# Order of the work in the attention slots of a hybrid encoder layer, on one Trainium2 core

## What is computed

```
h = RMSNorm(x);  P = h @ W_in, split into q,k,v of branch A; q,k,v of branch B; u of branch C; gate logits
A = softmax attention over a band of 9 chunks of 64 (here: all earlier chunks), relative bias,
    RMS-normed q and k, 8 heads of 64
B = stick-breaking attention, 8 heads of 64: w_ts = sig(z_ts) * prod_{s<j<t} (1 - sig(z_tj)), s < t
C = trailing means over 2/4/8/16 tokens of u, minus u, times a small matrix per group
x = x + W_out( sig(g_A)*(A W_a) + sig(g_B)*(B W_b) + sig(g_C)*(C W_c) )
x = x + W_down( silu(conv(hg)) * conv(hv) ),  [hg|hv] = RMSNorm(x) @ W_up
```

## Time and profile before

| | |
|---|---|
| median of 3 runs | 869.53 us (867.52 to 869.59) |
| the profiled execution | 869.46 us, its span in the trace 867.8 us |
| PE busy | 843.1 us (97%), 3953 matmuls |
| DVE, ACT, POOL busy | 522.5, 388.7, 138.3 us |
| granted TensorE clock, mean | 0.998 |
| DMA | 81.5 MB, mean 94 GB/s |
| slots 0 to 7 and the tail | from about 73 to 345 us of the span |

### The profile page before, as it was taken

The page is one execution under the profiler, slowest core; times in us unless marked ns, Lnnn a source line. Parts: engine busy times, 40 slices in busy tenths (PEclk is TensorE's granted clock), DMA queues, the critical chain, the costliest instruction groups (busy, mean ns, idle before and its releaser), DMA issues.

```text
span 867.8 us, 11900 instructions
## 1 busy us (share of the span) xinstructions
PE 843.1 (97%) x3953; PEld 693.1 (80%) x3953; DVE 522.5 (60%) x715; ACT 388.7 (45%) x557; POOL 138.3 (16%) x118
## 2 busy tenths in 40 slices
PE   5999999999999988999999999999999999999998
PEld 5788777787787777888888888888888888888886
DVE  5435768767467577455554666666666667533334
ACT  6435776655645535343435454333333334322221
POOL 2200222200100133000000312222222222200000
PEclk9999999999999999999999999999999999999999
DMA  6333223221312322333334332333333333222223
GB/s 199 99 97 98 68 78 98 75 71 49 97 48 69 89 72 86 99 93 99 97 95 135 97 97 78 96 96 96 96 96 96 97 96 96 98 97 96 97 97 121
DMA packets 126634, 81.50 MB, mean 94 GB/s; under 512 B 5028, under 2 KB 116360, under 8 KB 126608
## 3 DMA queue, kind: packets, MB, share of 16 engines
q1 hardware_dynamic: 125936, 79.04, 30.1%
q0 software_dynamic: 672, 2.12, 1.0%
HBM read 79.03 MB, written 2.12 MB: 94 GB/s over the span
## 4 chain that ended last, share of the span: by engine, by line
PE 83%; DVE 9%; ACT 3%; issue 2%; POOL 1%; DMA 1%; SPq 1%; ACTq 0%; DVEq 0%; POOLq 0%
PE ps L1182 25%; PE ps L1184 25%; PE ps L1183 25%; DVE suffix L909 2%; PE ps L1257 1%; PE ps L1269 1%; DVE pt_lo L932 1%; PE ps L1283 1%; PE ps L1284 1%; DMA w_raw<-in_w_in_dram 1%; DVE pa L916 1%; PE ps L1236 1%; DVE w_lo L799 1%; DVE out_sb L1172 1%; POOL o_lo L381 1%
## 5 line engine op out<-in xcount | busy, mean ns | idle before, releaser
L799 DVE TENSOR_TENSOR w_lo<-w_raw,w_hi 128x1024 fp32r<-128x1024 f32 x141 | 175.4, 1244 | 182.0 <-ACT w_hi L463 142.7
L1182 PE MATMUL ps<-h_lo,w_hi 128*128 128x512 f32 x704 | 277.4, 394 | 1.4 <-ACT gates L576 0.6
L1184 PE MATMUL ps<-h_hi,w_lo 128*128 128x512 f32 x704 | 274.2, 389 | 0.0
L1183 PE MATMUL ps<-h_hi,w_hi 128*128 128x512 f32 x704 | 274.1, 389 | 0.0
L463 ACT ACTIVATE w_hi<-w_raw 128x1024 fp32r<-128x1024 f32 x126 | 133.6, 1060 | 313.3 <-PE ps L1184 313.2
L1182 PEld LDWEIGHTS ps<-h_lo,w_hi 128*128 128x128 f32 x704 | 132.2, 188 | 28.9 <-issue 2.2
L1184 PEld LDWEIGHTS ps<-h_hi,w_lo 128*128 128x128 f32 x704 | 132.2, 188 | 28.0
L1183 PEld LDWEIGHTS ps<-h_hi,w_hi 128*128 128x128 f32 x704 | 132.3, 188 | 26.5 <-issue 0.2
L1182 PE MATMUL ps<-w_lo,a_hi 128*128 128x512 f32 x176 | 68.5, 389 | 0.0
L1183 PE MATMUL ps<-w_hi,a_hi 128*128 128x512 f32 x176 | 68.5, 389 | 0.0
L1184 PE MATMUL ps<-w_hi,a_lo 128*128 128x512 f32 x176 | 68.5, 389 | 0.0
(11 more groups left out here) (186 smaller groups left out, 1125.3 us busy)
## 6 DMA issues: line engine op xcount, KB each, us to landing
w_raw<-in_w_in_dram SPq DMA_DIRECT2D x104, 256.0 KB, 3.1
w_raw<-in_w_up_dram SPq DMA_DIRECT2D x88, 256.0 KB, 3.1
w_raw<-in_w_down_dram SPq DMA_DIRECT2D x44, 256.0 KB, 2.8
w_raw<-in_w_out_dram SPq DMA_DIRECT2D x16, 256.0 KB, 3.0
x_in<-in_x_dram SPq DMA_DIRECT2D x4, 512.0 KB, 6.3
bias_rev<-rel_bias_rows POOLq DMA_DIRECT2D x8, 256.0 KB, 3.5
x_re<-in_x_dram SPq DMA_DIRECT2D x2, 1024.0 KB, 6.0
w_raw<-in_w_branch_a_dram SPq DMA_DIRECT2D x8, 256.0 KB, 2.7
```

Source lines behind the costliest of these rows:

```text
L799: v.tensor_tensor(w_lo[:, slot, :], w_raw[:, slot, :], r32(w_hi[:, slot, :]), ALU.subtract)\
L1182: mm3(dst, l_hi, r_lo, start=start, stop=False, **kw)
L1183: mm3(dst, l_hi, r_hi, start=False, stop=False, **kw)
L1184: return mm3(dst, l_lo, r_hi, start=False, stop=stop, **kw)
```

## The change

- `o_sum` has a half for each head; `o_part(s, h)` waits for the `o_lo` of the same head one slot earlier.
- TensorE, stick-breaking slots: head 0's transposes stand in the middle of tile b+1, head 0's output and head 1's transposes in the middle of b+2, head 1's output in the middle of b+3. Softmax slots keep their order.
- All slots: the wait for the second gate of the slot before stands ahead of tile b+1 instead of tile b.
- The masks of a slot's scores are added ahead of all scores, not behind each block.
- The split of a slot's values is done at the end of the slot before, by ACT and DVE. ACT's gate copy stands ahead of the rounding of b+5.
- DVE: `sticks` becomes `stick_scan` and `stick_weights`; the second weights come behind the second scan, `lo(b+2)` and head 0's `pt_lo`. The second softmax scaling stands ahead of `pt_lo`, head 0's sum ahead of the Newton steps. ACT's `o_part(s, 0)` stands ahead of `norms_a`.
- POOL begins the pooling sums only when all sixteen heads' weights are done (`p_ready` 16). In the tail mix 0 and 1 follow tile b+4, mix 2 and 3 tile b+5, and `pooled_lo` is a function of its own.
- ACT's and DVE's loops over slots 1 and 2 are written out, and the table preload before ACT's is gone.

The diff, without the changed indices of `o_sum` in other lines and without functions that were only split:

```diff
-            ("o_sum", [P, S], FP32))
+            ("o_sum", [P, 2, S], FP32))
...
                 pool.wait_ge(o_hi_ready, s * 2 + h + 1)
-                pool.tensor_tensor(o_lo[own(h), s, :], o_sum[own(h), :], r32(o_hi[own(h), s, :]), ALU.subtract)\
+                pool.tensor_tensor(o_lo[own(h), s, :], o_sum[own(h), h, :], r32(o_hi[own(h), s, :]), ALU.subtract)\
...
+            pool.wait_ge(p_ready, 16)
             step = 0
...
+            def v_split_hi(s, v, pair):
+                if not (isinstance(s, int) and s == 0):
                     a.wait_ge(pv_done, s * 2)
...
             def o_part(s, h):
                 a.wait_ge(pv_done, s * 2 + h + 1)
-                if not (isinstance(s, int) and s + h == 0):
-                    a.wait_ge(o_lo_ready, s * 2 + h)
-                act(o_sum[own(1 - h), :], ps[own(1 - h), HEAD[h], :], ACT.Copy).then_inc(o_part_ready, 1)
+                if not (isinstance(s, int) and s == 0):
+                    a.wait_ge(o_lo_ready, s * 2 + (h - 1))
+                act(o_sum[own(1 - h), h, :], ps[own(1 - h), HEAD[h], :], ACT.Copy).then_inc(o_part_ready, 1)
...
-            def slot(s, attn, proj):
+            def slot_a(s, proj):
                 b = s * 4 + N_SLOT
...
-                first = isinstance(s, int) and s == 0
-                if attn == "A":
-                    v_split_hi(s, v_a, s, first)
-                    attn_probs(s, 0, attn)
-                    attn_probs(s, 1, attn)
-                else:
-                    attn_probs(s, 0, attn)
-                    attn_probs(s, 1, attn)
-                    v_split_hi(s, v_b, s - 4, False)
+                first = s == 0
                 t = s * 2 + 2
-                if attn == "A":
-                    pt_split_hi(s, 0, first)
+                attn_probs(s, 0, "A")
+                attn_probs(s, 1, "A")
+                pt_split_hi(s, 0, first)
...
-                if attn == "B":
-                    pt_split_hi(s, 0, first)
                 hi_at(b + 2, 0, half + 1)
                 if proj == "A":
                     proj_a(t + 1, 1, PROJ[1], b + 2, True)
+                    o_part(s, 0)
                     norms_a(t, HEAD[0] + 1)
-                elif proj == "B":
...
+                    o_part(s, 0)
                 pt_split_hi(s, 1, False)
                 hi_at(b + 3, 1, half + 1)
-                o_part(s, 0)
+                o_split_hi(s, 0)
                 hi_at(b + 4, 0, half + 2)
                 gate_store(s * 2, PROJ[0], b + 3)
+                o_part(s, 1)
                 if proj == "A":
                     hat_hi(t, 0)
+                    hat_hi(t + 1, 1)
+                o_split_hi(s, 1)
+                if proj == "A":
+                    v_split_hi(s + 1, v_a, s + 1)
+                else:
+                    v_split_hi(s + 1, v_b, s - 3)
+                gate_store(s * 2 + 1, PROJ[1], b + 4)
+                hi_at(b + 5, 1, half + 2)
+            def slot_b(s):
+                b = s * 4 + N_SLOT
+                half = s * 2 + N_SLOT // 2
+                attn_probs(s, 0, "B")
+                attn_probs(s, 1, "B")
+                a.wait_ge(unit_done, b + 1)
+                act(qk_hi[:, 0, :], ps[:, PROJ[0], :], ACT.Copy).then_inc(qk_hi_ready, 1)
+                hi_at(b + 2, 0, half + 1)
+                pt_split_hi(s, 0, False)
...
+                pt_split_hi(s, 1, False)
                 o_split_hi(s, 0)
-                if proj == "A":
-                    hat_hi(t + 1, 1)
+                hi_at(b + 4, 0, half + 2)
+                gate_store(s * 2, PROJ[0], b + 3)
                 o_part(s, 1)
                 o_split_hi(s, 1)
+                v_split_hi(s + 1, v_b, s - 3)
+                gate_store(s * 2 + 1, PROJ[1], b + 4)
                 hi_at(b + 5, 1, half + 2)
-                gate_store(s * 2 + 1, PROJ[1], b + 4)
-            slot(0, "A", "A")
-            a.preload_act_table_set("natural_log_exp_and_others")
-            with a.Fori(1, 3) as s:
-                slot(s, "A", "A")
-            slot(3, "A", "B")
+            v_split_hi(0, v_a, 0)
+            for s in range(3):
+                slot_a(s, "A")
+            slot_a(3, "B")
             a.preload_act_table(ACT.Sigmoid)
             with a.Fori(4, 7) as s:
-                slot(s, "B", "B")
+                slot_b(s)
...
             u_store(0, PROJ[0])
+            hi_at(b + 2, 0, half + 1)
             pt_split_hi(s, 0, False)
-            hi_at(b + 2, 0, half + 1)
             u_store(1, PROJ[1])
+            hi_at(b + 3, 1, half + 1)
+            o_part(s, 0)
             pt_split_hi(s, 1, False)
-            hi_at(b + 3, 1, half + 1)
+            o_split_hi(s, 0)
...
-            o_part(s, 0)
-            o_split_hi(s, 0)
-            pl_hi_split(0)
             hi_at(b + 4, 0, half + 2)
             u_store(2, PROJ[0])
+            pl_hi_split(0)
             o_part(s, 1)
             o_split_hi(s, 1)
             pl_hi_split(1)
+            u_store(3, PROJ[1])
             hi_at(b + 5, 1, half + 2)
-            u_store(3, PROJ[1])
+            gate_store(14, PROJ[0], b + 5)
+            hi(b + 6, 0)
             pl_hi_split(2)
             pl_hi_split(3)
-            hi(b + 6, 0)
-            gate_store(14, PROJ[0], b + 5)
-            for i in range(3):
-                oc_split_hi(i)
+            oc_split_hi(0)
+            oc_split_hi(1)
+            gate_store(15, PROJ[1], b + 6)
             hi(b + 7, 1)
-            gate_store(15, PROJ[1], b + 6)
+            oc_split_hi(2)
             oc_split_hi(3)
...
-                if attn == "A":
-                    d.wait_ge(s_done, s + 1)
-                    d.wait_ge(bias_ready, s * 2 + 2)
-                    if not first:
-                        d.wait_ge(t_done, s * 2)
-                    v_split_lo(s, v_a, s)
-                    softmax_logits(s, 0)
-                    softmax_scale(s, 0)
-                    softmax_logits(s, 1)
-                else:
-                    sticks(s, 0)
-                    v_split_lo(s, v_b, s - 4)
-                    sticks(s, 1)
+                d.wait_ge(s_done, s + 1)
+                d.wait_ge(bias_ready, s * 2 + 2)
+                if s:
+                    d.wait_ge(t_done, s * 2)
+                softmax_logits(s, 0)
+                softmax_scale(s, 0)
+                softmax_logits(s, 1)
+                softmax_scale(s, 1)
                 pt_split_lo(s, 0)
-                if attn == "A":
-                    softmax_scale(s, 1)
                 if proj == "B":
                     raw_lo(t, 0)
                 lo(b + 2, 0)
                 if proj == "B":
                     raw_lo(t + 1, 1)
+                o_sum_up(s, 0)
                 if proj == "A":
                     newton_half_q(s + 1)
                 pt_split_lo(s, 1)
                 lo(b + 3, 1)
-                o_sum_up(s, 0)
...
                 o_sum_up(s, 1)
                 lo(b + 4, 0)
+                if proj == "A":
+                    v_split_lo(s + 1, v_a, s + 1)
+                else:
+                    v_split_lo(s + 1, v_b, s - 3)
                 lo(b + 5, 1)
-            slot(0, "A", "A")
-            with d.Fori(1, 3) as s:
-                slot(s, "A", "A")
-            slot(3, "A", "B")
+            def slot_b(s):
+                b = s * 4 + N_SLOT
+                t = s * 2 + 2
+                stick_scan(s, 0)
+                stick_weights(s, 0)
+                stick_scan(s, 1)
+                raw_lo(t, 0)
+                lo(b + 2, 0)
+                pt_split_lo(s, 0)
+                stick_weights(s, 1)
+                raw_lo(t + 1, 1)
+                lo(b + 3, 1)
+                o_sum_up(s, 0)
+                pt_split_lo(s, 1)
+                lo(b + 4, 0)
+                o_sum_up(s, 1)
+                v_split_lo(s + 1, v_b, s - 3)
+                lo(b + 5, 1)
+            v_split_lo(0, v_a, 0)
+            for s in range(3):
+                slot_a(s, "A")
+            slot_a(3, "B")
...
             s, b = 7, N_SLOT + 28
-            sticks(s, 0)
-            v_split_lo(s, v_b, 3)
+            d.wait_ge(v_lo_ready, 8)
             v.memset(u_pad[:, :, 0:16], 0.0).then_inc(u_init, 1)
-            sticks(s, 1)
+            stick_scan(s, 0)
+            stick_weights(s, 0)
+            stick_scan(s, 1)
+            lo(b + 2, 0)
             pt_split_lo(s, 0)
-            lo(b + 2, 0)
+            stick_weights(s, 1)
+            lo(b + 3, 1)
+            o_sum_up(s, 0)
             pt_split_lo(s, 1)
...
-            o_sum_up(s, 0)
             pooled(0)
             lo(b + 4, 0)
+            pooled_lo(0)
             o_sum_up(s, 1)
             pooled(1)
+            pooled_lo(1)
             lo(b + 5, 1)
             pooled(2)
+            lo(b + 6, 0)
+            pooled_lo(2)
             pooled(3)
-            lo(b + 6, 0)
-            for i in range(3):
-                oc_split_lo(i)
+            pooled_lo(3)
+            oc_split_lo(0)
+            oc_split_lo(1)
```

(78 more changed lines are left out.)

24 lines of the change are left out of this document (12 added, 12 removed).

## The result

| | before | after |
|---|---|---|
| median of 5 runs | 869.59 us (867.52 to 870.16) | 849.35 us (849.22 to 850.05) |
| ratio | | 0.9774, 95% interval 0.9763 to 0.9784 |
| profiled execution, span | 869.46, 867.8 us | 850.05, 848.4 us |
| first scores of slot 0 to the first matmul of the merge | 73.11 to 344.67: 271.56 us | 73.21 to 325.25: 252.04 us |

The kernel is 20.2 us faster, 2.3%; the forecast was 18.3 us (851.2 us, range 848.2 to 857.5). All of it lies between slot 0 and the merge: 19.5 us there against 19.4 us of the span.

A forecast was written before the change was run, and what follows sets the result against it. TensorE, busy 843.1 of 867.8 us, was taken to bound the kernel, its slot waits coming from late DVE or ACT work. Gains summed to 18.3 us: 869.46 - 18.3 = 851.2 us, range 848.2 to 857.5.

The forecast's parts named there:

- Masks: Scores of the four stick-breaking slots: masks put together at the front save 4 x 0.5 = 2.0 us.
- near the pairs: Eight masks in a row taken as 0.85 us, between ends of 0.5 and 1.8; two take 0.21 up to the next kind.
- Slots 4 to 6: Heads half a tile later: `pa` waits go (3.1 us over slots 4 to 7), output products start earlier (0.8 in 4 to 6).
- Slot 7 and tail: POOL's later sums shorten head 1's scans (3.6 us), the clock recovers (1.7), mix 2 behind tile b+5 saves 2.4.
- Boundaries, 2.2 us: Boundaries of slots 0-1, 1-2, 2-3: a sum buffer per head takes POOL out and the wait goes, 2.2 us.
- Scores to tile, 0.9 us: Slots 1 to 3: moving the last gate's wait from tile b to b+1 saves 0.9 us.
- Slot 1's softmax, 1.15 us: Table reload and value splits leave the start of the slot, so 0.98 us of idle and 0.16 go: 1.15 us.
- The sums' new place: Pooling sums now lie over DVE's `lo(b+3)`, first output sum and `pt_lo`: 0.85 us charged to `lo`, none to `pt_lo`.
- rival 1: DVE's chain in the softmax slots is late after all; 3 to 4 us of gain stay away, about 855; chance 0.2.
- the second: Rival: pooling sums come too late, so mix 1 or tile b+5 waits for `pl_lo` or `lo(b+5)`; about 854 us; chance 0.15.
- The third: Rival: waits only move, each slot being bound by ACT and DVE, not their order; 868 to 871 us; chance 0.03.
- The fourth, the clock: Not among the prediction's three listed rivals; its expected sign was a granted clock of 1.00 throughout the slots.

The follow-up runs named there:

- experiment 2: Kernel before with only POOL's wait for the last weights added: 864.71 us, ratio 0.9952; conversely, changed kernel without that wait: 851.19 us, ratio 0.9791.
- experiment 6: Kernel before with only TensorE's new order: 887.38 us, ratio 1.0226 (the slower order); conversely, changed kernel with heads' work between tiles again: 852.53 us.

## Why the prediction was right, and where it was not

The direction, the range and the mechanism held: the waits went away, slot by slot, and no new one of a microsecond took their place. Going through its steps:

- **Masks: the term that was mis-sized.** 2.0 us in the sum, 3.5 by the experiments from both sides (4 x 0.88). I took 0.85 us for eight masks in a row; they take 0.55, near the cheap end that the prediction had at 0.5. The step that failed is "near the pairs": in a row a pair takes 0.14 us, so 0.07 of its 0.21 was a change of kind. The sum also left out the 0.09 us ahead of the scores. The miss of 1.5 us is larger than the whole difference between 18.3 and 19.5 us; others of the opposite sign (the softmax slots below) make up for part of it, so that the total came so near is in part luck.
- **Slots 4 to 6.** Expected 0.8 + 0.26 + 0.5 a slot, measured 2.1: 0.88 for the masks, 1.06 for the two waits as forecast, and the 0.15 that is left for the slower first matmuls behind a wait, which the prediction left out of the sum and put into the range. Undoing the part in the changed kernel returned 3.2 us where 3.9 were forecast.
- **Slot 7 and tail.** 3.6 + 1.7 + 2.4 + 0.8 for the transposes' wait + 0.5 for the masks = 9.0 expected, 9.14 measured. Its biggest part was tested by itself: 3.6 + 1.7 = 5.3 expected, 4.9 found, the rest being 0.27 us ahead of the output that stay in the old order (0.50 after the tile's last matmul where 0.23 is the pitch). The new place of the mixes (2.4) was not undone by itself.
- **Boundaries, 2.2 us:** the size was right, the reason was not. "A buffer per head takes POOL out" is not what did it: with one buffer no wait returns, and with two in the old order none goes. The prediction had the order too (head 0's sum ahead of the Newton steps), but only as what follows next. It expected 0.3 us to spare; the second sum ends 0.22 before the scores.
- **Scores to tile, 0.9 us:** the same: the moved wait is not needed; what is left as the reason is ACT's order.
- **Slot 1's softmax, 1.15 us:** the wait went, less 0.15. "About half a microsecond of slack" was wrong: there is none. The values' place is worth nothing, since POOL's `o_lo` holds them at their new one, and the reload alone is covered. With 0.15 us missing in each of slots 1 to 3 the softmax slots gave 4.1 us instead of 4.7.
- **The sums' new place.** `pt_lo` stayed at 1.49 us in every run, also right beside POOL's additions, as the row and the rule of the Trainium skill (SBUF — State Buffer, Who interferes with whom) had it. I charged 0.85 us to a `w_lo`; POOL's addition was lengthened in its stead, by 0.9.
- **The high end of the range.** By the prediction's own terms rivals 1 and 2 together give 857.8 us, and the dearest masks with rival 1 858.8; it wrote 857.5. The result lies far from it.

Of the rivals, the first came true by 0.15 us a slot; the second by one wait of 0.2 us ahead of tile b+5 (0.43 us after mix 1 instead of 0.23). The third (waits only move) is excluded for the whole change, but it is exactly what TensorE's part alone does, and more. The fourth, the clock, did not happen in mid-tile: 1.00 in all of slots 4 to 7. The fall of the clock that the prediction tied to the wait of 3.5 us is borne out in the profiled executions: without that wait there is none (experiment 2), and in the slower order of experiment 6 there is one around the 5.36 us of idle (0.50, that is 1.2 GHz, over 322 to 326) and one around the 3.08 us ahead of the third mix (0.50 over 352 to 356). But one of three waits of 2.61 us was followed by it as well, and executions that were not profiled have a mean clock of 0.998 without the long wait, or of 1.000 with it. So the 1.7 us are what a fall cost here (4.0 x 0.43), not what every such wait costs.

What stays open: which of the moves in DVE's and ACT's softmax order carries the boundaries (head 0's sum, its rounding, or both); whether reload and values together would bring slot 1's wait back; and what the mixes' new place and slot 3's `lo(b+2)` gave, which no experiment undid. The parts undone one at a time in the changed kernel return 3.5 + 1.6 + 3.2 + 0.1 = 8.4 of the 19.5 us. The rest is covered by more than one part at once, or belongs to the order as a whole.

## What to carry to other kernels

When one engine is busy for 97% and the rest waits in fractions of a microsecond, work on due times: write down when each piece is due and done, and move consumers later and producers' queues into the order of the due times together; the consumer's move alone cost 18 us here. Look at what a third engine does to a producer's duration: one wait on POOL, keeping it off DVE's scans, was worth 4.9 us in the old order (and 1.6 in the new one). And put matmuls of one kind together: six fewer changes between bf16 masks and float32 scores saved 0.9 us a slot, without anything else being moved.

## What was not expected of the hardware

- Eight bf16 matmuls of 128 columns in a row take 0.55 us, 0.07 each; each of six changes between them and the scores' matmuls on 64 rows costs about 0.13 us on average ((3.40 - 2.61) / 6). The masks differ from the scores in number format and in rows (128 against 64); no run tells the two apart.
- Which engine is held when DVE and POOL meet differs. Scans of two SBUF inputs went from 2.97 to 5.4 us beside POOL's additions; a `w_lo` of 1.23 us that had begun 0.14 us before an addition kept its length and the addition went from about 1.1 to 2.02. With the sums late in the old order (experiment 2) a `w_lo` that began 0.21 us after an addition took 1.92.
- TensorE's clock fell after it had resumed, not during the wait, in four of the six falls seen: after 3.5 us of idle in three profiled executions of the old DVE order, and after one of three waits of 2.61 us.
- A wait of TensorE need not be printed: 0.15 us before the transposes in the softmax slots show only as a start that is 0.38 after the last matmul where the pitch is 0.23.
